# Forgetting attention on one core: masked rough tiles inside masked exact tiles, four rough tiles a round, and GpSimd makes the first head's second add in rounds without masks

## The reference, cut to what matters

```python
for blk in range(seq // B_BLOCK):
    logits = (einsum('bhqd,bhkd->bhqk', q[:, :, s0:s1], k[:, :, :s1])
              + log_f_cum[:, :, s0:s1, None] - log_f_cum[:, :, None, :s1])
    causal = arange(s0, s1)[:, None] >= arange(s1)[None, :]
    p = softmax(where(causal, logits, -inf), axis=-1)
    outs.append(einsum('bhqk,bhkd->bhqd', p, v[:, :, :s1]))
```

## Time and profile before

| | |
|---|---|
| median of three runs | 3289.4 us (3288.13 to 3299.26) |
| the profiled execution | 3294.57 us, its span 3293.0 us |
| granted clock, mean over the span | 0.967 |
| TensorE matmuls busy | 3068.8 us (93%) |
| VectorE, ScalarE, GpSimd busy | 1743.8, 1238.0, 1040.6 us |

### The profile page before, as it was taken

How to read it: one execution, slowest core, us unless ns; L and a number is a source line. 1 busy time by engine, 2 the same in 40 slices (tenths; PEclk the granted TensorE clock), 3 DMA queues, 4 the chain that set the end, 5 groups by cost and what they waited for, 6 DMA issues and landing times.

```text
span 3293.0 us, 40380 instructions
## 1 busy us (share of the span) xinstructions
PE 3068.8 (93%) x15148; PEld 2306.6 (70%) x15148; DVE 1743.8 (53%) x2715; ACT 1238.0 (38%) x2162; POOL 1040.6 (32%) x729
## 2 busy tenths in 40 slices
PE   5999899999987998895899999999999999999998
PEld 3766667888876887684787888887555555555587
DVE  4555564558464666554422222102677777778633
ACT  4245445544413544323422211220344444445411
POOL 0488980223215552110000000001354454555400
PEclk8999999999998999897999999999899999999999
DMA  5243431576746563655443432116345333431243
GB/s 219 66 130 113 127 117 52 167 231 190 243 107 213 188 212 124 208 178 170 136 124 103 128 106 77 71 48 163 97 94 132 84 90 87 116 87 40 88 149 122
DMA packets 274165, 427.93 MB, mean 130 GB/s; under 512 B 74127, under 2 KB 171031, under 8 KB 268845
## 3 DMA queue, kind: packets, MB, share of 16 engines
q1 hardware_dynamic: 239804, 341.36, 35.2%
q0 software_dynamic: 18064, 68.25, 6.6%
q10 hardware_dynamic: 16112, 15.86, 1.6%
HBM read 274.58 MB, written 150.69 MB: 129 GB/s over the span
## 4 chain that ended last, share of the span: by engine, by line
PE 47%; DVE 2%; ACT 1%; ACTq 1%; DMA 1%; SPq 1%; issue 1%; DVEq 0%
PE at_ps L1979 7%; PE at_ps L2017 5%; PE at_ps L1882 5%; PE at_ps L1884 5%; PE at_ps L1883 5%; PE at_ps L1961 4%; PE at_ps L1964 4%; PE at_ps L1947 3%; PE at_ps L1895 2%; PE at_ps L1896 2%; PE at_ps L1897 2%; PE at_ps L1993 1%; ACTq L2362 1%; DMA at_parts<-s_xnT 1%; ACT at_probs L2433 0%
## 5 line engine op out<-in xcount | busy, mean ns | idle before, releaser
L2433 ACT ACTIVATE at_probs<-at_ps 128x512 f32<-128x512 f32 (+3 forms) x640 | 331.3, 534 | 349.6 <-PE at_ps L1964 284.8
L2161 DVE TENSOR_REDUCE at_partial<-at_ps 128x1 f32<-128x512 f32 (+3 forms) x640 | 371.3, 605 | 147.5 <-PE at_ps L1947 114.6
L106 PE MATMUL pa_y<-pa_h_high,pa_w_high 128*128 128x512 f32 x1056 | 422.2, 400 | 11.2 <-ACT pa_acc L772 5.4
L108 PE MATMUL pa_y<-pa_h_high,pa_w_low 128*128 128x512 f32 x1056 | 413.2, 391 | 0.0
L107 PE MATMUL pa_y<-pa_h_low,pa_w_high 128*128 128x512 f32 x1056 | 413.0, 391 | 0.0
L1707 POOL TENSOR_TENSOR at_plain<-at_plain,at_probs 128x512 f32<-128x512 f32 (+3 forms) x256 | 310.0, 1211 | 226.5 <-ACT at_probs L2433 210.9
L1882 PE MATMUL at_ps<-at_h_high,at_w_high 128*128 128x512 f32 x768 | 301.8, 393 | 30.0 <-DVE at_w_low L2091 28.2
L1883 PE MATMUL at_ps<-at_h_low,at_w_high 128*128 128x512 f32 x768 | 300.8, 392 | 0.0
L1884 PE MATMUL at_ps<-at_h_high,at_w_low 128*128 128x512 f32 x768 | 300.5, 391 | 0.0
L1961 PE MATMUL at_ps<-at_h_low,at_h_high 67*128 67x512 f32 (+3 forms) x640 | 261.8, 409 | 12.0 <-ACT at_probs L2433 11.9
L1964 PE MATMUL at_ps<-at_h_low,at_h_high 128*128 128x512 f32 (+3 forms) x640 | 254.4, 398 | 0.0
(11 more groups left out here) (348 smaller groups left out, 5509.6 us busy)
## 6 DMA issues: line engine op xcount, KB each, us to landing
at_h_low<-s_Q SPq DMA_DIRECT2D x96, 256.0 KB, 7.2
s_qkv<-pa_sil POOLq DMA_DIRECT2D x16, 1024.0 KB, 6.6
pa_sil<-s_qkv SPq DMA_DIRECT2D x16, 1024.0 KB, 6.3
dr_kv<-s_qkv SPq DMA_DIRECT2D x16, 1024.0 KB, 8.7
s_K<-at_parts SPq DMA_DIRECT2D x64, 256.0 KB, 4.2
s_Q<-at_parts SPq DMA_DIRECT2D x64, 256.0 KB, 4.1
at_h_high<-s_K SPq DMA_DIRECT2D x32, 512.0 KB, 5.6
pa_wraw<-in_a_w_in_dram ACTq DMA_DIRECT2D x15, 1024.0 KB, 6.0
```

What stands on the lines that cost most here:

```text
L106: nc.tensor.matmul(out, w_high[:, k], h_high[:, k], start=k == 0, stop=False)
L108: ins = nc.tensor.matmul(out, w_low[:, k], h_high[:, k], start=False, stop=k == KC - 1)
L2161: reduced.done(v.tensor_reduce(partial[:, u % 2, h * NQ + sub, grp:grp + 1], rough[:, j % 3, 0:width], AX.X, ALU.max))
L2433: probs_ok.done(a.activation(probs[:, R % 2, t, h, off:BLK], logits[:, l % 3, off:BLK], ACT.Exp))
```

## The change

It has four parts. (1) `ITEMS` is cut into `whole(u)` (no mask, from the last key group to the first) and `masked(u)`. The first 64 now run in the eight slots, eight each: the masked of units 0 and 1, and the whole of units 1 to 3. (2) Rounds take four or none: masked rough tiles in a unit's last two rounds, whole ones in the others once round 6 is passed, none in rounds 2, 3, 6, 143 to 145, 148 to 151 and from 154 on. (3) In a masked exact tile the rough tile stands between K1 and its mask, and the two masks stand side by side. (4) In 72 rounds (`shared`: neither a unit's first nor its last two) GpSimd makes the first head's second add as well, and VectorE only the first. The first rough tile of each group of keys now waits for its own block and the unit's own.

```diff
+    def whole(u):
+        return [(u, h, sub, grp) for grp in reversed(range(UNITS[u][1])) for h in range(2) for sub in range(NQ)]
+    def masked(u):
+        return [(u, h, sub, UNITS[u][1]) for h in range(2) for sub in range(NQ)]
     EARLY = 8
-    PER_TILE = ITEM_END[2] // EARLY
+    ITEMS = masked(0) + whole(1) + masked(1) + whole(2) + whole(3)
+    PER_TILE = len(ITEMS) // EARLY
...
+    wholes = [x for u in range(NB, len(UNITS)) for x in whole(u)]
+    maskeds = [x for u in range(2, len(UNITS)) for x in masked(u)]
     for R in range(ROUNDS):
-        due = [(ITEM_END[u] - DONE, max(START[u] - 4, 0)) for u in range(len(UNITS)) if ITEM_END[u] > DONE]
-        take = max([-(-n // (d - R + 1)) for n, d in due if d >= R], default=0)
+        of = maskeds if R >= START[UNIT_OF[R] + 1] - 2 else wholes if R > START[2] else []
+        ROUGHS[R] = range(len(ITEMS), len(ITEMS) + min(4, len(of)))
+        ITEMS += of[:4]
...
+        def shared(R):
+            return START[UNIT_OF[R]] < R < START[UNIT_OF[R] + 1] - 2
...
                     for t, off in ((0, off_a), (1, off_b)):
+                        if t == 1 and shared(R):
+                            probs_ok.wait(pool, 4 * R + 2)
+                            v_summed.wait(pool, n)
+                            both = sum_v[:, u % 2]
+                            v_summed.done(g_.tensor_tensor(both, both, probs[:, R % 2, 1, 0], ALU.add))
...
             def rough_logits(j):
                 u, h, sub, grp = ITEMS[j]
                 p, qb = UNITS[u]
-                if j == 0 or ITEMS[j - 1][0] != u:
-                    for n in range(qb + 1):
+                if h == 0 and sub == 0:
+                    for n in (grp, qb):
                         pe.wait_ge(one_in[p % 2][n], (p // 2 + 1) * ONE)
...
+            def mask_rough(j):
+                u, h, sub, grp = ITEMS[j]
+                if grp == UNITS[u][1]:
+                    rough_ok.done(mm(rough[:, j % 3, sub * P:(sub + 1) * P], ident_b[:, :], mask_q[:, :], start=False, stop=True))
...
                 mm(out, K1[s][0:DH + 3, h, k_at], Q1[s][0:DH + 3, h, q_at], start=True, stop=False)
                 if kb >= qb * NQ:
+                    for j in beside:
+                        rough_logits(j)
                     mm(logits[:, l % 3, off:off + P], ident_b[:, :], mask_k[:, :], start=False, stop=False)
+                    for j in beside:
+                        mask_rough(j)
                 logits_ok.done(mm(out, K2[s][:, h, k_at], Q2[s][:, h, q_at], start=False, stop=True))
+                if kb < qb * NQ:
+                    for j in beside:
+                        rough_logits(j)
```

More of the change, by code:

```diff
@@ L2053, in _ @@
                         pe.wait_ge(top_in, 32 * (u + 1))
-                    part = -(-len(items) // 4)
                     for t, kb, off in tiles(R):
                         for h in range(2):
-                            exact_logits(R, t, kb, off, h)
-                            for j in items[(2 * t + h) * part:(2 * t + h + 1) * part]:
-                                rough_logits(j)
+                            exact_logits(R, t, kb, off, h, items[2 * t + h:2 * t + h + 1])
                 if R == ROUNDS:
@@ L2157, in reduce @@
                 width = BLK if grp < qb else (sub + 1) * P
-                if j == 0 or ITEMS[j - 1][0] != u:
-                    top_ok.wait(dve, u - 2)
+                if j == UNIT_BEGIN[u]:
+                    top_ok.wait(dve, u - 2 * NB)
                 rough_ok.wait(dve, j)
-                reduced.done(v.tensor_reduce(partial[:, u % 2, h * NQ + sub, grp:grp + 1], rough[:, j % 3, 0:width], AX.X, ALU.max))
-                if j == ITEM_END[u] - 1:
+                reduced.done(v.tensor_reduce(partial[:, u % (2 * NB), h * NQ + sub, grp:grp + 1], rough[:, j % 3, 0:width], AX.X, ALU.max))
+                if j == UNIT_END[u]:
                     reduced.wait(dve, j)
                     turned_ok.wait(dve, u - 2)
-                    top_ok.done(v.tensor_reduce(top[:, u % 2], partial[:, u % 2, :, 0:qb + 1], AX.X, ALU.max))
+                    top_ok.done(v.tensor_reduce(top[:, u % 2], partial[:, u % (2 * NB), :, 0:qb + 1], AX.X, ALU.max))
             make_columns(0)
@@ L2284, in _ @@
                         first_two(R)
-                    else:
+                    elif not shared(R):
                         add_up(R, 1)
```

19 lines of the change are left out of this document (8 added, 11 removed).

## The result

| | before | after |
|---|---|---|
| median | 3289.4 us (3286.5 to 3301.5, 7 runs) | 3312.9 us (3307.2 to 3317.1, 7 runs) |
| ratio to the kernel before | | 1.0064, 95% interval 1.0047 to 1.0080 |
| profiled execution, span | 3294.57, 3293.0 us | 3314.7, 3312.8 us |

What follows compares the result with a forecast made beforehand. TensorE's own matmul work was taken to bound the rounds. Terms of -8.8 - 4.0 + 9.1 + 6.3 - 1 + 1.5 summed to +3.1 us on 3289.4, about 3293 us; range 3274 to 3312.

Steps and rivals of the forecast that it cites:

- Nested masks: Masked rounds: side-by-side masks save 0.08 us at 158 rough masks, less 3.8 for narrow K1; -8.8 us.
- Four or none a round: Rounds: 24 whole rough tiles move to the slots, 8 masked ones come in; -4.0 us.
- Tops: Transposed tops in ScalarE's queue: as many as before, but ahead of other, less often narrow rounds; -1 us.
- Eight in a slot: Eight early slots: two more tiles each wait on VectorE's reductions, clock behind slots as now; +9.1 us.
- The step of 1.35 us for each of the six wide bursts: Early slots: two more wide tiles add 1.35 us in each of six slots holding only wide tiles.
- A fetch that is asked for earlier: Round 23: TensorE waits 6.1 us for block 2's gates, the present wait in round 28 goes; +6.3 us.
- I add 0.8 for a lower clock after the gap: Round 23: 0.8 us more for TensorE's lower clock behind the wait for the gates.
- Adds on GpSimd: 72 shared rounds: VectorE's relief is worth nothing, GpSimd's lateness in six rounds mostly covered; +1.5 us, bounds 0 and +36.
- the clock's: Early slots: longer, under half load, they bring two low-clock stretches each instead of one; +11, 3304 us; chance 13%.
- VectorE's: Rounds: VectorE paces them, so 72 shared rounds gain 0.15 us each, -11; 3274 us or less; chance 17%.
- GpSimd's: Shared rounds: GpSimd paces them, its lateness growing and holding up rough matmuls; +22, 3314 us; chance 12%.
- The masks' own: Masked tiles: a mask behind a mask costs like one before a matmul; 3302 to 3306 us; chance 10%.

Runs made afterwards that it cites:

- e4: Changed kernel with each masked rough tile and its mask behind K2 again, as before the change: 3326.2 us, ratio 1.0100.
- e5: Kernel before with only the nesting of masked rough tiles added; its slots, tile order and adds stay: 3289.0 us, ratio 0.9999.
- e11: e9 with the output weights' subtraction also left out of masked rounds that have rough tiles: 3306.6 us, ratio 1.0042.
- e1: Changed kernel with keys, queries and gates of all four blocks issued ahead of their other parts: 3305.0 us, ratio 1.0036.
- e3: Changed kernel without GpSimd's added share; VectorE makes all adds of the first head again: 3311.5 us, ratio 1.0065.
- e9: Changed kernel with only the output weights' preparation left out of rounds behind a turned top: 3316.1 us, ratio 1.0068.
- e10: Changed kernel with ten early slots of four rough tiles, output weights' preparation skipping rounds behind a turned top and begun one round later: 3276.0 us, ratio 0.9948.
- e2: Changed kernel with six rough tiles in each early slot instead of eight, the rest of unit 3 in rounds from 2 on: 3308.1 us, ratio 1.0049.
- e6: e2 with the output weights' preparation left out of rounds behind a turned top: 3298.0 us, ratio 1.0024.

## Why the prediction came out as it did

The sum was +3.1 us; the medians say +23.5 and the two profiled spans +19.8. Of the 16.7 us between sum and spans, the last pair is 7.1, the rounds' smaller gain 4.3 (9.5 for 13.8), round 23 3.6 and the slots 2.5; GpSimd's 1.5 did not come, and 0.8 is the unchanged first stretch. The large misses all have the same sign, so nothing made up for them.

*Nested masks*, -8.8: the size held inside this change (12 us by e4), the picture behind it did not. The price of 0.08 was read from one shape, that of the earlier trace rows, and this shape saves nothing: it stayed at 0.58. Four other shapes do save 0.07 to 0.08. The count was wrong too. Of the 232 rough masks before, 109 stand last in a round and not 74, which leaves 123; but those that stand last save as well (0.96 to 0.85 us), and the narrow K1 that was to cost 0.06 saves 0.07. That these errors cancel in part is luck. The second mask starts 0.067 us behind the first (median of 240), 0.012 more than the 0.055 counted, about 3 us over all. That is below the 81 ns of the Trainium skill (TensorE: Matmul & The Clock Gate, Back-to-back issue gap); of the 6 us that the prediction worked out from this rule, half came. Nesting alone, on the order of before, gives nothing that can be measured (e5).

*Four or none a round*, -4.0, and *Tops*, -1: together with the nest they were to give 13.8. Measured are 9.5 (pair 0 2.3; pair 1 1.5, leaving out round 23's 9.9 us; pairs 2 to 6 4.4; the last 1.3 in e11). With the nest at 12, nothing is left for these two. e4, which is the new order without the nest, shows it directly: leaving out round 23 in both, its pairs 0 to 6 sum to 3.4 us more than before, though they hold five rough tiles fewer. So the step that failed here is that fewer tiles were taken for less time. Which part of the new order takes it back is open.

*Eight in a slot*, +9.1, measured +11.6 by the profiles. The bursts account for 11.1 of it (34.2 us for eight, against 23.1), the tiles between them for 0.5: the clock behind a slot moved little, as assumed. The step of 1.35 us for each of the six wide bursts was right at the full clock: 4.32 us in e1 against 2.98 on average for the same slots before (17.9 together). In the changed profile they measure 4.58 to 4.67 (the longest with a transposed top in it), 27.7 together, since the clock is at its lower level at their ends; this 0.3 each is what the term lacked. It also lacked that the clock in the slots is not a constant. The six profiles with these slots (changed, e1, e3, e4, e9, e11) have 80.0 to 83.3 us at 0.83 to 0.87; the two with the slots of before have 71.5 at 0.86 and 61.9 at 1.00. So the price of this part is between 8 and 21 us, and how often the kernel before runs like e5, these profiles don't tell.

*A fetch that is asked for earlier*, +6.3, measured +9.9 in round 23: place, releaser and mechanism as said. The wait was 6.88 for 6.1. The step that failed is "I add 0.8 for a lower clock after the gap": it was 4.0 (15.71 - 4.87 - 6.88), because the lower level lasted the whole rest of the round. It holds in all five profiles with this fetch: the clock adds 3.4 to 4.0 us, whether the wait is 3.4 or 6.9 (e11: 3.78, and 12.08 for the round). That this profile's wait is near the 6.1 forecast is partly chance.

*Adds on GpSimd*, +1.5 with a worst case of 36: right where it was worked out. The chain is 4.5 us for 4.65, and e3 shows that the share costs and brings nothing in unmasked rounds. By the Trainium skill (SBUF — State Buffer, SBUF: two separate sides) GpSimd and two-input VectorE operations shut each other out. The trace agrees: 1.67 us for VectorE's add begun behind GpSimd's, 0.68 for one begun alone, and in the last pair 2.25 for a GpSimd add of 1.27.

*What was missing.* No term dealt with the last pair except GpSimd's lateness. It lost 7.1 us against e11's 99.1; up to 3.4 of them are the clock (an estimate: half of the 6.8 us at the lower level in rounds 147 to 149), and e11 has no such time in this pair. The change emptied rounds 143 to 145 and put four rough tiles each into 146 and 147, and it moved the tops to rounds 141, 148 and 154. Both then met the output weights' preparation, which stood in rounds 142 to 150 before and after. That is the largest part of the error: the order of *all* instructions in these rounds was not read, only the order of those that the diff moves.

The rivals: the clock's (slower by up to 11, two low stretches behind each slot) named the right effect and the wrong place. The tiles between the slots have 21.6 us at the lower level, against 20.0 before; the clock acted at the ends of the bursts, behind round 23's gap and in the last pair. VectorE's and GpSimd's both fell by e3. The masks' own (a mask behind a mask costs like one ahead of a matmul) fell by e4.

## What to carry to other kernels

When a table of work is levelled to "four or none", look at what else stands at fixed rounds: a once-only job of 2 us placed ahead of the short reductions cost 0.8 to 3.0 us in a round with four rough tiles (152 in e10, 147 in the change), and the same job in a quieter round costs nothing. A producer that fills three banks ahead of a slower consumer should be given bursts of about as many tiles as banks, in more places (four tiles for three banks here; three were not tried). Before pricing a step that recurs in several shapes, read it in each of them. Price a TensorE gap at its own length and that of the work behind it at half the clock, for as long as rows of the same kernel show the clock low behind such a gap.

## What was not expected of the hardware

A gap of 6.88 us was followed by 7.3 us at a granted clock of 0.51, and one of 3.78 (e11) by 3.4 us more than the gap in the same round; in e2 a round with 1.8 us of idle time (busy 7.42 of 9.20) was followed by one of 9.2 us at 0.51, with TensorE busy all through it. The same eight slots of six tiles ran at a mean of 0.86 (before) and 1.00 (e5), 71.5 and 61.9 us; with other six tiles each they ran at 0.92 (e2) and 0.90 (e6), 67.1 and 68.6 us. A VectorE subtraction of 128x1024 took 1.22 us alone and 2.31 beside GpSimd's adds, and GpSimd's add of 128x512 1.27 and 2.25.
